# Turn of a pair of heads in a new order: transposes and gating before rotations, key weights before values

## The reference

```python
q      = (cq @ w_uq) -> 16 heads of 128 plain + 64 rotary columns; the rotary ones are rotated by position
k, v   = c @ w_uk, c @ w_uv             # 128 columns per head, from the shared latent c
s      = (q k^T + q_rope k_rope^T) * ATTN_SCALE, masked by chunks of 64
o      = softmax(s) v
out    = (o * silu(gate)) @ w_out_b ;  y = LayerNorm(ALPHA * x + out)
```

## Time and profile before

| | |
|---|---|
| median of three runs | 2071.39 us |
| profiled execution | 2074.88 us |
| its span | 2072.8 us |
| busy in the span: TensorE, VectorE, ScalarE, GpSimd | 94%, 54%, 35%, 22% |
| mean granted clock of TensorE | 0.977 |
| heads stage, from the front of the first pair to the requests | about 1015 to 1680 us |
| one steady pair | 81.8 us |

### The profile page before, as it was taken

How to read it: one execution, slowest core, us unless ns; L and a number is a source line. 1 busy time by engine, 2 the same in 40 slices (tenths; PEclk the granted TensorE clock), 3 DMA queues, 4 the chain that set the end, 5 groups by cost and what they waited for, 6 DMA issues and landing times.

```text
span 2072.8 us, 31540 instructions
## 1 busy us (share of the span) xinstructions
PE 1942.7 (94%) x11755; PEld 1827.9 (88%) x11755; DVE 1115.9 (54%) x1964; ACT 720.1 (35%) x1247; POOL 462.7 (22%) x390
## 2 busy tenths in 40 slices
PE   6999999999869999999799999999999959999997
PEld 6999999999748899999789988988989859988886
DVE  3365555645657512422466766666667546763643
ACT  3333233323221121212253453443544447762100
POOL 0121222212212110000144443443444410000111
PEclk9999999999989999999899999999999979999999
DMA  5121122211174211233111121112011053354421
GB/s 161 41 74 44 40 73 63 63 32 54 34 248 129 74 51 65 78 115 112 38 43 47 40 59 46 37 46 62 29 49 41 28 132 90 90 210 154 137 92 41
DMA packets 190337, 158.78 MB, mean 77 GB/s; under 512 B 36176, under 2 KB 174928, under 8 KB 190000
## 3 DMA queue, kind: packets, MB, share of 16 engines
q1 hardware_dynamic: 184608, 137.31, 21.7%
q10 hardware_dynamic: 5184, 18.88, 2.6%
q0 software_dynamic: 464, 1.48, 0.2%
HBM read 115.78 MB, written 41.84 MB: 76 GB/s over the span
## 4 chain that ended last, share of the span: by engine, by line
PE 51%; DVE 7%; issue 6%; ACT 4%; DMA 2%; POOL 2%; SPq 0%; DVEq 0%; ACTq 0%; POOLq 0%
PE ps L118 15%; PE ps L120 15%; PE ps L119 15%; POOL h_p L1613 1%; PE ps L1726 1%; DVE h_mx L1930 1%; DVE h_p L1889 1%; PE ps L1709 1%; PE ps L1708 1%; ACT h_p L1829 1%; DMA s_qr_raw<-scratch_qr 1%; DVE h_pt_l L112 1%; DMA m_w_raw<-in_w_out_a 1%; DVE s_mx L2495 1%; DVE h_kt_l L112 1%
## 5 line engine op out<-in xcount | busy, mean ns | idle before, releaser
L1622 POOL TENSOR_SCALAR h_p<-h_p,h_rsum 128x128 f32<-128x128 f32 (+7 forms) x128 | 221.0, 1728 | 304.0 <-DVE h_rsum L1934 303.9
L118 PE MATMUL a_pj<-act_h,a_w_l 128*128 128x384 f32 x768 | 277.2, 361 | 7.8 <-DVE act_l L112 7.8
L119 PE MATMUL a_pj<-act_l,a_w_h 128*128 128x384 f32 x768 | 261.9, 341 | 0.0
L120 PE MATMUL a_pj<-act_h,a_w_h 128*128 128x384 f32 x768 | 261.8, 341 | 0.0
L1829 ACT ACTIVATE h_p<-ps,h_mx 128x128 f32<-128x128 f32 (+7 forms) x128 | 95.0, 742 | 219.9 <-DVE h_mx L1930 219.9
L118 PE MATMUL ps<-act_h,m_c_l 128*128 128x384 f32 x480 | 163.6, 341 | 4.4 <-DVE act_l L112 2.4
L120 PE MATMUL ps<-act_h,m_c_h 128*128 128x384 f32 x480 | 163.2, 340 | 0.0
L119 PE MATMUL ps<-act_l,m_c_h 128*128 128x384 f32 x480 | 163.2, 340 | 0.0
L112 DVE TENSOR_TENSOR h_pt_l<-ps,h_pt_h 128x128 fp32r<-128x128 f32 (+2 forms) x192 | 100.9, 553 | 113.8 <-ACT h_pt_h L107 110.4
L118 PEld LDWEIGHTS a_pj<-act_h,a_w_l 128*128 128x128 f32 x768 | 146.0, 190 | 13.0 <-DVE act_l L112 8.5
L119 PEld LDWEIGHTS a_pj<-act_l,a_w_h 128*128 128x128 f32 x768 | 146.0, 190 | 3.4 <-issue 3.4
(11 more groups left out here) (325 smaller groups left out, 4925.5 us busy)
## 6 DMA issues: line engine op xcount, KB each, us to landing
a_w_raw<-in_w_in_a SPq DMA_DIRECT2D x32, 512.0 KB, 4.1
m_c_raw<-in_w_in_b SPq DMA_DIRECT2D x20, 512.0 KB, 4.2
scratch_gate<-m_sg SPq DMA_DIRECT2D x16, 576.0 KB, 5.2
h_gate<-scratch_gate SPq DMA_DIRECT2D x64, 128.0 KB, 2.1
scratch_og<-h_gate SPq DMA_DIRECT2D x64, 128.0 KB, 1.7
o_w_raw<-in_w_out_b SPq DMA_DIRECT2D x16, 512.0 KB, 7.7
o_g_raw<-scratch_og SPq DMA_DIRECT2D x24, 256.0 KB, 4.3
a_factors<-in_x SPq DMA_DIRECT2D x9, 512.0 KB, 5.2
```

Source lines behind the costliest of these rows:

```text
L118: nc.tensor.matmul(out, ll, rh, start=first, stop=False)
L119: nc.tensor.matmul(out, lh, rl, start=False, stop=False)
L120: return nc.tensor.matmul(out, lh, rh, start=False, stop=last)
L1622: nc.gpsimd.tensor_scalar(weights_of(u), weights_of(u), rsum[:, u % PB], None, ALU.mult).then_inc(S["p_ready"], 1)
```

## The change

- VectorE, at a turn: step 1 of the rotation is taken out of unit 15 and stands behind `gated(6)`, before low part 0 and step 2; low part 1 moves ahead of `gated(7)`.
- All engines: UT stands before V0, not between V1 and V2. Its count in `proj_out` and `proj_high` changes with it, and SyncE's load of the next pair's weights, which waits for UT, comes earlier.
- ScalarE, front of the first pair: the four zero fills stand before the rotary steps.
- Last pair: SyncE's first load for the requests stands in the round of block 3, not 4; GpSimd's zeroing for it after unit 8, not 10; ScalarE and VectorE split the first queries after all units (VectorE after `gated(6)`), not in unit 13.

```diff
--- before.py
+++ after.py
@@ -1431,7 +1431,7 @@
 TSTEPS = [(u, i, min(4, 2 * place_of(u)[2] + 2 - i)) for u in range(UNITS)
           for i in range(1 - unit(u)[1], 2 * place_of(u)[2] + 2, 4)]
 
-PROJ = ["QA0", "QA1", "KA0", "KA1", "QA2", "R0", "R1", "R2", "V0", "V1", "UT", "V2", "V3",
+PROJ = ["QA0", "QA1", "KA0", "KA1", "QA2", "R0", "R1", "R2", "UT", "V0", "V1", "V2", "V3",
         "KB0", "QB0", "KB1", "QB1", "QB2", "QL"]
 NP = len(PROJ)
 PLACE = {"R1": 0, "R2": 2, "V0": 3, "V1": 4, "V2": 5, "V3": 6}
@@ -1591,7 +1591,7 @@
                     sp.wait_ge(S["proj_out"], pr * NP + NP)
                     sp.dma_start(d["scratch_ql"][bass.ds(pr, 1)].rearrange("o p t -> p (o t)"), flat(qlat[:])).then_inc(S["ql_stored"], 16)
                     sp.dma_start(d["scratch_qr"][bass.ds(pr, 1)].rearrange("o p t -> p (o t)"), flat(qr[0:RD])).then_inc(S["qr_stored"], 16)
-                if g == 4 and last:
+                if g == 3 and last:
 
                     sp.wait_ge(S["ql_stored"], 16 * PAIRS)
                     sp.wait_ge(S["qr_stored"], 16 * PAIRS)
@@ -1620,7 +1620,7 @@
                 pool.wait_ge(S["inv_done"], pr * UNITS + u + 1)
                 pool.sem_inc(S["scale_go"], 1)
                 nc.gpsimd.tensor_scalar(weights_of(u), weights_of(u), rsum[:, u % PB], None, ALU.mult).then_inc(S["p_ready"], 1)
-                if last and u == 10:
+                if last and u == 8:
 
                     pool.wait_ge(S["proj_out"], PAIRS * NP)
                     k.samples.zero_first(pool)
@@ -1748,9 +1748,10 @@
         pe.wait_ge(S["zeroed"], 4)
 
         def body(pr, first, last):
-            proj(pr, "V0", first)
+            for s in ("UT", "V0"):
+                proj(pr, s, first)
             scores(pr, 0)
-            for s in ("V1", "UT", "V2", "V3"):
+            for s in ("V1", "V2", "V3"):
                 proj(pr, s, first)
             scores(pr, 1)
             scores(pr, 2)
@@ -1840,16 +1841,19 @@
                 q = slice(half * P, half * P + P)
                 round_high(nc, pt_h[G % 2][:, place:place + w, q], bank[:, 4 + i % TB, 0:w * P].rearrange("p (a q) -> p a q", a=w)).then_inc(S["t_high"], 1)
 
-        for s in PROJ[:NE] + ["R0", "R1", "R2"]:
+        for s in PROJ[:NE]:
             proj(0, s, True)
 
         for x in (pt_h[0], pt_h[1], pt_l[0], pt_l[1]):
             nc.scalar.activation(x[:, 0, 0:P], k.ident[:], ACT.Identity, scale=0.0).then_inc(S["zeroed"], 1)
+        for s in ("R0", "R1", "R2"):
+            proj(0, s, True)
 
         def body(pr, first, last):
-            proj(pr, "V0", first)
+            for s in ("UT", "V0"):
+                proj(pr, s, first)
             exp(pr, 0)
-            for s in ("V1", "UT", "V2", "V3"):
+            for s in ("V1", "V2", "V3"):
                 proj(pr, s, first)
             exp(pr, 1)
             exp(pr, 2)
@@ -1863,12 +1867,11 @@
                 if u + 3 < UNITS:
                     exp(pr, u + 3)
                 turned(pr, u)
-                if last and u == 13:
-                    k.samples.first_queries_high(act)
             if not last:
                 for s in ("R0", "R1", "R2"):
                     proj(pr + 1, s, False)
             else:
+                k.samples.first_queries_high(act)
                 k.samples.first_keys_high(act)
         pairs(act, body)
 
@@ -1977,9 +1981,9 @@
                     inverted(pr, u + 2)
                 if u in BESIDE and not (last and BESIDE[u][1]):
                     s, n = BESIDE[u]
-                    if s[0] == "R":
-                        rope(pr + 1, int(s[1]), False)
-                    else:
+                    if s == "R0":
+                        rope(pr + 1, 0, False)
+                    elif s[0] != "R":
                         proj(pr + n, s, first and not n)
                 if u + 3 < UNITS:
                     largest(pr, u + 3)
@@ -1989,16 +1993,16 @@
                     for i in SPLITS[u]:
                         split_low(dve, pr + 1, i)
                 turned(pr, u)
-                if last and u == 13:
-                    k.samples.first_queries_low(dve)
             gated(pr, NG - 2)
             if not last:
+                rope(pr + 1, 1, False)
                 rope_third(pr + 1, False)
+                rope_low(pr + 1, 1)
             else:
+                k.samples.first_queries_low(dve)
                 k.samples.first_keys_low(dve)
             gated(pr, NG - 1)
             if not last:
-                rope_low(pr + 1, 1)
                 rope_low(pr + 1, 2)
         pairs(dve, body)
```

## The result

Twenty executions of the changed kernel have a median of 2076.26 us (2072.73 to 2079.26), twenty of the kernel before, beside them, 2072.66 us (2070.01 to 2076.02). The ratio is 1.0016, 95% interval 1.0009 to 1.0023. So the change costs 3.6 us (1.9 to 4.8). The profiled execution took 2076.51 us.

The account below looks back on a forecast made before the run. TensorE is busy nearly throughout, so only its gaps count, held at turns by VectorE's chain. Turns +15.6, fills -6.6 and last pair -3.3 gave +5.7 us on the median 2071.39: 2077 us, range 2066 to 2086.

Parts of the forecast that it names:

- slower by over 0.2%: Whole kernel: outcome slower by more than 4.1 us, what a measurement can tell from no change; chance 0.66.
- within: Whole kernel: outcome within 0.2% (4.1 us) of the kernel before; chance 0.20.
- The turn: Seven turns between pairs: VectorE's new order +2.52 us, key weights first -0.28; +2.2 each (1.6 to 2.7), +15.6 in all.
- The low part's place: VectorE at a turn: low part of step 0, now beside GpSimd's adds, takes 1.73 us as in the first pair, not 1.06.
- Key weights first: VectorE at a turn: the gap before V2 and V3 goes, -0.28 us a turn (bounds 0 and -0.3).
- The fills: Front of first pair: fills wait for nothing, second maximum comes at 1030.6 instead of 1037.23; -6.6 us (bounds -3.4 and -6.6).
- The last pair: End of heads stage: 13.15 us wait goes, but block 6's gate load queues behind the requests' load; -3.3 us (-5.5 to -1).
- Rival C: Every turn: gaps of 3.5 us put TensorE's clock down, +1 us a turn, 2084 us; chance 0.11.
- that of the fourth block: Sign in the steady turn: a TensorE wait near 1.8 us before the fourth score block.

Follow-up runs that it names:

- e1: Kernel before with only VectorE's new turn (step 1 behind the gating of block 6, low part 1 ahead of that of block 7): 2089.66 us, ratio 1.0086.
- e2: Changed kernel with VectorE's turn put back to the old order, the other parts kept: 2059.42 us, ratio 0.9931.
- e3: Changed kernel with the low part of rotary step 0 taken before step 1 on VectorE: 2073.36 us, ratio 1.0001.
- e7: Kernel before with only the four zero fills put before the rotary steps on ScalarE: 2064.78 us, ratio 0.9964.
- e4: Changed kernel with the second request's load issued only behind the gate load of block 7: 2072.36 us, ratio 0.9993.

## Why the prediction was right

Its time was 2077 us, measured 2076.26; its difference +5.7 us, measured +3.6 (1.9 to 4.8) in the runs and +4.55 in the traces. So the difference was 1 to 2 us too high, and part of the agreement of the times comes from the kernel before, whose median over twenty runs is 1.3 us above that of the three it was added to. Inside the sum two misses have opposite signs: the turns came out 0.85 us dearer than forecast, the last pair 1.9 cheaper. That the sum is nearer than its worst term is luck. And the sum was held for more certain than it should be: +5.7 is only 1.6 us above the bound of 4.1 us, yet "slower by over 0.2%" had 0.66 and "within" 0.20. The measured ratio lies within, with an interval over both.

- *The turn, +2.24 each, +15.6 in all.* Measured 16.45, and 2.26 in the steady pairs (84.10 against 81.84). Step by step: idle time before the gating 1.9 forecast, 2.06 measured; low part 1.73 and 1.75; wait for V0 about 3.5 and 3.46; pair 84 and 84.1 us. e1 and e2 put the price at 17.0 and 16.8 with this part alone taken in or out. The two terms of a turn missed by little, and against each other: the new order costs 2.64 in e1's trace (84.48 less 81.84) where 2.52 was forecast, and the key weights give more than forecast (below).
- *The low part's place.* The forecast took the first pair's row and not the steady one, because its neighbours were the same. e3 shows this choice to be right: 0.95 without the add beside it, 1.75 with it. The Trainium skill's rule ("SBUF — State Buffer", section "SBUF: two separate sides") agrees in kind; the estimate of 1.85 from it was 0.1 too high.
- *Key weights first, -0.28.* e2 gives -0.37. The new wait on ScalarE, which the forecast feared, shows in the changed kernel as no cost: VectorE takes V1 to V3 in one group (1279.08, 1.89), without the gap before V2.
- *The fills, -6.6.* Measured -6.56, and -6.2 in e7's trace. The path after it is as forecast: V0 right behind the last rotary third, the second maximum 4.43 us later. The timelines of VectorE and of TensorE at the front:

```profile
1014.03 1.73 DVE L1905 SCALAR_TENSOR_TENSOR h_rq<-h_p,h_rq 64x768 fp32r<-64x768 f32 x1 [0.15 <-ACT h_rq L1801]
...
1022.60 0.95 DVE L1905 SCALAR_TENSOR_TENSOR h_rq<-h_p,h_rq 64x768 fp32r<-64x768 f32 x1 [2.09 <-ACT h_rq L1801]
1023.59 0.69 DVE L112 TENSOR_TENSOR h_v_l<-ps,h_v_h 128x512 fp32r<-128x512 f32 x1
...
1028.02 0.82 DVE L1933 TENSOR_REDUCE h_mx<-ps 128x1 f32<-128x640 f32 x1
```

```profile
1024.33 0.42 PE L118 MATMUL ps<-h_kt_h,h_qn_l 128*128 128x320 f32 x1 [1.80 <-DVE h_v_l L112]
...
1029.81 0.53 PE L118 MATMUL ps<-h_kt_h,h_qn_l 128*128 128x384 f32 x1 [1.76 <-ACT h_p L1830]
```

- TensorE's one wait of 11.26 us is gone. In its place stand three short ones at the front, 1.9 for the last rotary third (`h_rq` in the view of waits) and the 1.80 and 1.76 us above.
- *The last pair, -3.3 (bounds -5.5 and -1).* Measured -5.19. This is the term that was mis-sized. SyncE's issues, VectorE's gating of block 6 and TensorE's waits in the last pair, against the earlier trace rows:

```profile
1658.72 0.34 SPq L1576 DMA_DIRECT2D h_gate<-scratch_gate  x1
1659.17 0.40 SPq L2122 DMA_DIRECT2D s_ql_raw<-scratch_ql  x1
...
1680.77 0.42 SPq L1587 DMA_DIRECT2D scratch_og<-h_gate  x1
1683.10 0.35 SPq L1576 DMA_DIRECT2D h_gate<-scratch_gate  x1
```

```profile
1685.19 0.42 DVE L1951 TENSOR_TENSOR h_gate<-ps,h_gate 128x256 f32<-128x256 f32 x1 [9.37 <-DMA h_gate<-scratch_gate]
```

```profile
1678.13 3.28 PE L2187 MATMUL ps<-ident,h_w_raw 128*128 128x128 f32 x16 [2.25 <-issue]
...
1685.76 0.55 PE L118 MATMUL ps<-h_pt_h,h_v_l 128*128 128x256 f32 x1 [2.81 <-DVE h_gate L1951]
...
1690.70 0.40 PE L118 MATMUL ps<-s_ct_h,s_q_l 128*128 128x352 f32 x1 [0.49 <-issue]
```

- The mechanism was right: the gate load of block 6 waits behind the requests' load (1659.17 to 1680.77), and the gating for it, 9.37 us. But the issuing took 21.6 us, not 22.8, the store's landing 2.33, not 2.63, and from the gating to the first scores it took 5.5, not 5.9. With the gate load 0.1 quicker and the load starting 0.1 later behind it, that is the 1.8 us between the forecast (1685.3 less 1688.65) and -5.19. TensorE's 13.15 us became three waits, 2.25, 2.81 and 0.49.
- *Rival C, +1 a turn.* Its cause was real and its price was not: the clock fell at six of seven turns, but the matmuls that it slowed lie ahead of a wait for the exponential that had the room. It cost time in three places. At the front it lay over the fourth block, and at the turns of 1109 and 1361 over everything from the second block to the fourth (6.28 and 6.32 us, 5.3 at the others): these pairs took 84.79, 84.28 and 84.33 us, the others 84.05 to 84.10. That is 1.1 us over the whole stage, where the rival had 7. The forecast should have had this as a small part of itself.
- *What the rival's rows did not say.* The prediction finds the low clock once among the turns of the kernel before, in the first. It was there a second time: behind the wait of 1.90 us at 1366.07 the clock was at 0.54 from 1366 to 1368, the matmuls of the fourth block took 0.53 us each, and the pair took 82.64 us and not 81.84. So the seven turns' 16.45 us are 7x2.26=15.8, plus 1.1 for the low clock after the change, less 0.8 for the one before it, plus 0.3 for a first pair that was short before (81.54).
- *What was to show it:* all of the signs came, but that of the fourth block, where some 1.8 us were forecast in every turn; 1.60 stands in the turn at full clock, 0.33 in the last, and elsewhere slow matmuls fill the place.

## What to carry to other kernels

Releasing a waiting engine earlier is worth something only if the chain of the engine that releases it doesn't end later for it. Take the moment at which the chain hands over its last product, before and after, and count the idle stretch that the moved work leaves behind. Don't add up waits of TensorE when its clock can change, since slow matmuls pass for busy ones; set the moments of one marker per round side by side. And before small loads are moved ahead in a hardware queue's order, ask how long the issuing takes and which tiny, urgent load then stands behind it.

## What the runs showed of the hardware that was not expected

- TensorE's clock after the same wait of 3.46 us was at the low level in one turn (0.50 over the window) and full in another (1.00), in one execution. Before the first pair's fourth block, which ran at the low clock (0.57), stood waits of only 1.80 and 1.76 us, and in the kernel before the same wait of 1.90 us before the fourth block was followed by the low clock in one turn and not in the others (0.54 at 1366, 1.00 at 1284). The work between is the same by the program. What decides it is open.
- SyncE's issue of a load of small rows can itself be long. The loads of the requests' rows from `out_krope_sample` and `out_ckv_sample` held SyncE 0.68 to 5.06 us each, while a gate load takes 0.34; six of them are 16.9 of the 21.6 us for two requests. The first two (4.50 and 5.06 us) are the dearest, though the second request's are loads of the same shape (0.68 and 2.32). One request alone takes 14.2 us (e4). Why the first are dear isn't shown.
- Executions of one kernel lay as far apart as 8 us here (e3 2067.97 to 2076.26, e4 2066.58 to 2074.71), with mean granted clocks from 0.975 to 0.983. That is more than the 2.9 and 3.9 us by which their medians differ from the change's, so a single execution could have misled.
